# A hybrid layer's cache compression: ScalarE's work around a change of batch redistributed, and one addition moved to GpSimd

## The chip, the cores and the metric

The kernel runs on one core of a Trainium2 chip. The metric is the device time of one execution in microseconds, the median of three runs.

## The reference

The kernel computes one layer for a prompt of 1024 tokens and for 8 batches of 4 new tokens each, with a cache of 4096 past tokens. The layer has an HGRN2 mixer (a gated scan in chunks, 4 heads), a sparse attention (compressed blocks, selected blocks, window) and a feed-forward part with a convolution. What the change touches is the compression of cached keys and values, and the scan that runs beside it:

```python
def compress_rows(rows, pe, w1, w2):      # rows: (B, S, 2 groups, 64)
    ch = rows.reshape(B, n_chunks, 16, G, D)
    proj = jnp.einsum('bnsgd,psdh->pbngh', ch, w1)        # p: 2 halves of a block of 32
    bias = jnp.einsum('psd,psdh->ph', pe, w1)
    h = proj[0, :, 0:n_blk] + bias[0]
    h = h + proj[1, :, 1:1 + n_blk] + bias[1]
    return jnp.einsum('bngh,hd->bngd', jax.nn.silu(h), w2)

# the scan, in each chunk (C tokens), a = cumsum(log f):
att = einsum('bhtk,bhsk,bhtsk->bhts', q, k, exp(a_t - a_s))     # causal
o = att @ v + (q * exp(a)) @ s
s = exp(a_end) * s + (k * exp(a_end - a)).T @ v
```

## The kernel before, in words

The kernel is a sequence of stages. The one of this case is `compress_and_scan`. It has 72 steps: eight for each of the 8 batches of cached rows (64 steps, `PAIRS`), and eight for the prompt's rows. `at` is the step, `u = at // 8` the batch, `s = at % 8` the place in it. Each engine has its own program, written out by hand as a loop over the steps; semaphores tie them together. There is no planner.

In a step the engines prepare the data of step `at + 1` and TensorE multiplies those of step `at`:

- GpSimd gathers cached rows by an indirect DMA into one of 4 slots, three steps ahead (`gather`, line 2908).
- TensorE turns a slot into one bank, `pt`, three times (kinds 0 and 1: two halves of the rows to compress, kind 2: keys of the selection; line 3463). Each turn must wait until the bank is copied out.
- ScalarE and VectorE copy kind 0 out together (ScalarE two of four pieces, line 3156, VectorE two, `upper_copy`, line 3319), ScalarE copies kind 1 alone (four pieces, into `prow`). The result is `raw`. ScalarE then rounds it to a high part `XH` (line 3167), VectorE subtracts to get the low part `XL` (lines 3330 and 3332). For kind 0 the two halves of `raw` are also added in place (line 3333, VectorE) and split into `SH` (line 3175) and `SL`. For kind 2 the parts are `KTH` (line 3181) and `KTL` (line 3341), made by `keys`.
- TensorE runs `project_first` (with `XH`, `XL`, `SH`, `SL`), `project_second` in two halves, and `score`, into accumulators that are kept over the eight steps of a batch.

TensorE's order in a step is: turn 0 of the next step, `project_first`, turn 1, first half of `project_second`, `score`, turn 2, second half of `project_second`, with the products of the scan laid between. Turn 0 of step `at + 2` waits for the keys' low part of step `at + 1`.

At a change of batch, ScalarE copies the taps in step 7 (`keep_taps`, line 3115), VectorE joins them (`join_taps`, lines 3352 to 3354, six additions and subtractions that wait for each other), and in the next batch's step 0 ScalarE applies Silu: `hidden(u, 1)` straight from the accumulator, which TensorE needs before it may start the second projection, and `hidden(u, 0)` on the joined taps at the end of step 0 (both line 3132). Silu and Exp need a table load (1.28 us) whenever they take turns. In step 4 TensorE makes the compressed blocks (`blocks`, lines 3561 and 3568) into the bank of the scores, once ScalarE has copied the scores out (`keep_scores`, lines 3148 and 3149, every even step).

The scan takes one unit (a chunk of 128 tokens, or the new tokens) every two steps. GpSimd makes the differences of logarithms (`differences`, lines 2881 to 2885, 15 short instructions) and scales results (`scaled`), ScalarE takes exponentials (`exponentials`, odd steps), VectorE multiplies by keys and queries (`weigh`, part 0 at the end of an odd step, part 1 in the next even step), TensorE multiplies, VectorE masks and reduces (`pairs`, odd steps) to a tile `diag` of 128x32 whose four 32x32 blocks belong on the diagonal of `attT`. ScalarE copies them there (`diagonals`, line 3100), as its last work in the odd step; TensorE's `outputs` (line 3642), its last work in the odd step, waits for that.

SyncE stores values, loads the scan's chunks and, near the end of the stage, the next stage's tiles.

Of the kernel before, what the change touches and what calls it, by code (L numbers as in the profile page):

```python
# [2717 lines left out]
def compress_and_scan(nc, io, keep, scratch, consts_sb):  # L2718
# [11 lines left out]
    with ExitStack() as ctx:  # L2730
# [61 lines left out]
        raw_ready, upper_ready = [sem("raw_ready0"), sem("raw_ready1")], sem("upper_ready")  # L2792
        diag_kept = sem("diag_kept")
# [39 lines left out]

        def raw_whole(eng, at, k):
            eng.wait_ge(raw_ready[k], at + 1)
            if k == 0:
                eng.wait_ge(upper_ready, at + 1)
# [33 lines left out]
        def _(pool):  # L2871
# [38 lines left out]

            def add_scores(n):
                pool.wait_ge(s_kept, n + 1)
                nc.gpsimd.tensor_tensor(sx[:, n % 2, :], sx[:, n % 2, :], sxl[:], ALU.add).then_inc(s_added, 1)  # L2913

            differences(0)
            differences(1)
            pool.wait_ge(hc_in, 64)
            for at in range(LAST):
                if at + 3 < PAIRS:
                    gather(at + 3)  # L2920
                if at % 2 == 0:
                    if 2 <= at <= PAIRS:
                        add_scores(at // 2 - 1)
                    continue
                if at >= 2:
                    scaled(at // 2 - 1)
                if at // 2 + 2 < NN:
                    differences(at // 2 + 2)
# [148 lines left out]
        def _(act):  # L3077
# [16 lines left out]
            def diagonals(n):  # L3094
                if decode(n):
                    return
                act.wait_ge(a_kept, n + 1)
                for b in range(4):
                    x = slice(32 * b, 32 * b + 32)
                    last = nc.scalar.copy(attT[x, n % 2, x], diag[x, :])  # L3100
                last.then_inc(diag_kept, 1)

# [48 lines left out]
            def raw_copy(at, k):  # L3151
                act.wait_ge(t_ready[k], at + 1)
                if at >= 1:
                    act.wait_ge(l_ready[k], at)
                for g, a in parts[0:2] if k == 0 else parts:
                    last = nc.scalar.copy(part_of(raws[k], at, g, a), split(at, g, a))  # L3156
                last.then_inc(raw_ready[k], 1)
# [52 lines left out]
            for at in range(LAST):  # L3210
                u, s = at // NS, at % NS
                first_half(at + 1)
                if u >= 1 and s == 0:
                    hidden(u - 1, 1)
                if at % 2 == 0 and 2 <= at <= PAIRS:
                    keep_scores(at // 2 - 1)
                if s == NS - 1 and u < DB:
                    keep_taps(u)
                if at % 2 == 1 and at // 2 + 1 < NN:
                    exponentials(at // 2 + 1)  # L3220
                second_half(at + 1)
                if u >= 1 and s == 0:
                    hidden(u - 1, 0)
                if at % 2 == 1:
                    diagonals(at // 2)
                elif at >= 2:
                    squares(at // 2 - 1)
# [7 lines left out]
        def _(dve):  # L3235
# [24 lines left out]
            def pairs(n):  # L3260
# [12 lines left out]
                if n >= 1:  # L3273
                    dve.wait_ge(diag_kept, states(n - 1))
                nc.vector.tensor_reduce(diag[:], prod[:].rearrange("p l t -> p t l"), AX.X, ALU.add).then_inc(a_kept, 1)
# [34 lines left out]
            lows, boths = Steps(dve, low0_ready), Steps(dve, both_step)  # L3310

            def upper_copy(at):
                if at >= PAIRS:
                    return
                dve.wait_ge(t_ready[0], at + 1)
                if at >= 1:
                    dve.wait_ge(l_ready[0], at)
                for g, a in parts[2:4]:
                    last = nc.vector.tensor_copy(part_of(raws[0], at, g, a), split(at, g, a))
                last.then_inc(upper_ready, 1)  # L3320

            def low_part(at, k):
# [6 lines left out]
                elif k == 1:  # L3329
                    nc.vector.tensor_tensor(XL[:, at % 2, 1, :], raws[1], XH[:, at % 2, 1, :].bitcast(F32), ALU.subtract).then_inc(l_ready[1], 1)  # L3330
                else:
                    lows(nc.vector.tensor_tensor(XL[:, at % 2, 0, :], raw, XH[:, at % 2, 0, :].bitcast(F32), ALU.subtract))
                    nc.vector.tensor_tensor(raw[:, 0:256], raw[:, 0:256], raw[:, 256:512], ALU.add).then_inc(sum_ready, 1)
# [36 lines left out]
            upper_copy(0)  # L3370
# [31 lines left out]
            for at in range(LAST):  # L3402
                u, s = at // NS, at % NS
                n = at // 2
                if at + 1 < LAST:
                    upper_copy(at + 1)
                if at % 2 == 0:
                    if n >= 1 and not decode(n - 1):
                        results(n - 1)
                    weigh(n, 1)  # L3410
# [6 lines left out]
                if s == NS - 1 and u < DB:  # L3417
                    join_taps(u)
                if at + 1 < LAST:
                    low_part(at + 1, 1)  # L3420
                if at + 1 < PAIRS:
                    low_sum(at + 1)
                    keys(at + 1)
                if 1 <= u < DB - 1 and s == 1:
# [13 lines left out]
                if at % 2 == 1 and n + 1 < NN:  # L3438
# [8 lines left out]
        def _(pe):  # L3447
# [181 lines left out]
            def outputs(n):  # L3629
# [3 lines left out]
                pe.wait_ge(diag_kept, states(n))  # L3633
# [236 lines left out]
```

## Time and profile before

| | us |
|---|---|
| median of 3 runs | 2259.41 (2257.88 to 2262.35) |
| profiled execution, its own time | 2249.72 |
| its span | 2247.9 |
| TensorE busy (matmul) | 2066.3 |
| VectorE busy | 1441.2 |
| ScalarE busy | 1087.8 |
| GpSimd busy | 700.2 |

The span runs from the first to the last instruction of the profiled execution. The stage of this case lies between about 355 and 1041 us. A TensorE matmul's row has its duration in the pipeline; matmuls of 256 columns that follow each other start every 0.12 us.

### The profile page before, as it was taken

The numbers are of one execution on the slowest core, as the hardware profiler recorded it, in microseconds if no ns is written. First come the engines' busy times: TensorE is split into PE (matmuls) and PEld (weight loads), VectorE is DVE, ScalarE is ACT, GpSimd is POOL, SyncE is SP. The second block draws the span as 40 slices with busy tenths as digits, with TensorE's granted clock in tenths as the row PEclk, the third lists the DMA queues.
The fourth block names the chain that finished last, engine by engine and source line by source line (L and its number), as shares of the span: only waits on it lengthen the run. The fifth ranks groups of instructions, "written<-read, shape, count | busy, mean of one in ns | idle before, by whom it ended". The sixth has DMA issues, their size and how long they took to land. (4 is left out here: it accounts for less than half of the span.)

```text
span 2247.9 us, 44025 instructions
## 1 busy us (share of the span) xinstructions
PE 2066.3 (92%) x17158; PEld 1920.4 (85%) x17158; DVE 1441.2 (64%) x3058; ACT 1087.8 (48%) x2322; POOL 700.2 (31%) x996
## 2 busy tenths in 40 slices
PE   6999998998899889886789899898999999999997
PEld 5999997887888888874678777787999999999997
DVE  5212235776675766665678698548788788765567
ACT  4115214766766775764357487324333333334334
POOL 0001003655555654531059497120111111110000
PEclk9999999999999999976979899999999999999999
DMA  4115554765655655657610011331332332365352
GB/s 127 57 57 171 195 215 137 219 174 176 182 170 159 192 171 154 186 127 268 222 53 8 6 50 45 110 99 50 94 101 92 101 115 72 101 232 189 118 171 96
DMA packets 226055, 295.73 MB, mean 132 GB/s; under 512 B 23986, under 2 KB 161426, under 8 KB 224658
## 3 DMA queue, kind: packets, MB, share of 16 engines
q1 hardware_dynamic: 199224, 191.65, 28.1%
q0 software_dynamic: 26624, 101.27, 13.8%
q8 instruction: 137, 2.24, 0.4%
q14 instruction: 70, 0.57, 0.1%
HBM read 217.12 MB, written 82.63 MB: 133 GB/s over the span
## 5 line engine op out<-in xcount | busy, mean ns | idle before, releaser
L1568 POOL TENSOR_TENSOR C<-C,a_mt 128x264 f32<-128x264 f32 x66 | 69.3, 1070 | 404.1 <-ACT C L1653 270.4
L3520 PE MATMUL cplain<-a_XH,w1H 128*128 128x256 f32 x512 | 155.7, 304 | 12.2 <-ACT a_hs L3132 12.2
L2087 PE MATMUL f<-a_slot,wd_slot 128*128 128x264 f32 x1176 | 148.2, 285 | 2.0 <-DVE a_slot L1897 1.2
L2087 PEld LDWEIGHTS f<-a_slot,wd_slot 128*128 128x128 f32 x1176 | 144.8, 188 | 2.9 <-issue 1.9
L2050 PE MATMUL f<-a_b,ring 128*128 128x264 f32 x1056 | 144.1, 286 | 3.2 <-DVE a_b L1793 2.7
L3520 PE MATMUL cplain<-a_XL,w1H 128*128 128x256 f32 x512 | 145.0, 283 | 0.0
L3520 PE MATMUL cplain<-a_XH,w1L 128*128 128x256 f32 x512 | 144.6, 282 | 0.0
L3463 PE MATMUL cpt<-ident,X 128*128 128x128 f32 x768 | 119.1, 278 | 23.7 <-ACT a_prow L3156 19.5
L2050 PEld LDWEIGHTS f<-a_b,ring 128*128 128x128 f32 x1056 | 135.5, 190 | 3.8 <-issue 3.8
L502 PE MATMUL pj<-wH,xL 128*128 128x256 f32 (+2 forms) x464 | 130.9, 282 | 0.0
L502 PE MATMUL pj<-wH,xH 128*128 128x256 f32 (+2 forms) x464 | 130.8, 282 | 0.0
L502 PE MATMUL pj<-wL,xH 128*128 128x256 f32 (+2 forms) x464 | 130.5, 281 | 0.0
L2908 POOL DMA_INDIRECT X<-in_cache_nsa_kv,idx x122 | 118.6, 972 | 30.7 <-issue 25.0
L3463 PEld LDWEIGHTS cpt<-ident,X 128*128 128x128 f32 x768 | 88.2, 143 | 45.6 <-ACT a_prow L3156 36.1
L672 POOL TENSOR_SCALAR a_Prs<-a_Prs,a_cf 128x128 f32<-128x128 f32 (+7 forms) x64 | 110.5, 1746 | 17.0 <-DVE a_cf L817 16.9
L2050 PE MATMUL f<-b0a,ring 128*128 128x264 f32 x804 | 111.3, 289 | 1.5 <-ACT a_mt L1649 0.8
L3156 ACT COPY a_raw<-cpt 64x256 f32<-64x256 f32 x128 | 46.8, 366 | 132.9 <-PE cpt L3463 132.2
L3520 PEld LDWEIGHTS cplain<-a_XH,w1H 128*128 128x128 f32 x512 | 97.0, 189 | 15.0 <-issue 13.7
L2913 POOL TENSOR_TENSOR a_sx<-a_sx,a_sxl 64x512 f32<-64x512 f32 x32 | 48.3, 1511 | 196.1 <-ACT a_sxl L3149 196.1
L3156 ACT COPY a_prow<-cpt 64x256 f32<-64x256 f32 x256 | 93.6, 366 | 31.4 <-PE cpt L3463 28.6
L825 DVE TENSOR_TENSOR a_PTL<-pt,a_PTH 128x512 fp32r<-128x512 f32 x132 | 90.1, 688 | 28.1 <-ACT a_PTH L729 25.8
L2050 PE MATMUL f<-a_b,a_ring 128*128 128x264 f32 x792 | 106.7, 284 | 1.1 <-ACT a_mt L1649 0.6
(619 smaller groups left out, 6576.5 us busy)
## 6 DMA issues: line engine op xcount, KB each, us to landing
v_s<-X SPq DMA_DIRECT2D x64, 256.0 KB, 3.8
a_slot<-a_T SPq DMA_DIRECT2D x20, 792.0 KB, 4.6
raw<-in_w_in POOLq DMA_DIRECT2D x12, 1024.0 KB, 6.0
V<-v_s SPq DMA_DIRECT2D x6, 2048.0 KB, 11.2
raw<-in_w_gate SPq DMA_DIRECT2D x22, 512.0 KB, 5.2
raw_odd<-in_w_val SPq DMA_DIRECT2D x22, 512.0 KB, 5.6
a_T<-C SPq DMA_DIRECT2D x20, 528.0 KB, 3.2
a_T<-sums SPq DMA_DIRECT2D x11, 792.0 KB, 4.5
```

The costliest lines, as they stand in the source:

```text
L502: last = nc.tensor.matmul(bank[u % 8][0:r, 0:nw], xp[:, k, a * P:a * P + r], wp[:, j % 2, k, 0:nw], **flags)
L672: nc.gpsimd.tensor_scalar(Pr_of(u)[:, h, 0:u.w], Pr_of(u)[:, h, 0:u.w], cf[:, u.n, h:h + 1], None, ALU.mult).then_inc(p_ready, 1)
L825: nc.vector.tensor_tensor(lo, src, hi.bitcast(F32), ALU.subtract).then_inc(l_ready, 1)
L1568: nc.gpsimd.tensor_tensor(C[j][:, at], C[j][:, at], mt[:, q % 2, m, c], ALU.mult).then_inc(multiplied, 1)
L2050: last = nc.tensor.matmul(out_bank(q, r, c), w[:, k], x[:, k], start=begins and k + part == 0, stop=k == 3 and part == 2, skip_group_check ...
L2087: last = nc.tensor.matmul(acc(u, o, h), x(n)[:, k, P * o:P * o + P], a(n)[:, k, HW * h:HW * h + HW], start=u in (0, 2, 4, 6) and begins an ...
L2908: nc.gpsimd.indirect_dma_start(X[:, j % SLOTS, half].rearrange("p t n -> p (t n)"), None, cache, bass.IndirectOffsetOnAxis(ap=idx[:, j // ...
L2913: nc.gpsimd.tensor_tensor(sx[:, n % 2, :], sx[:, n % 2, :], sxl[:], ALU.add).then_inc(s_added, 1)
L3156: last = nc.scalar.copy(part_of(raws[k], at, g, a), split(at, g, a))
L3463: last = nc.tensor.transpose(pt[:, c:c + P], X[:, at % SLOTS, h, a, P * kind:P * kind + P], ident[:])
L3520: last = nc.tensor.matmul(out[:, h], w, x, start=(begins and q + h + part == 0), stop=(ends and q + h == 2 and part == 2), skip_group_chec ...
```

## The change

- The four copies of the diagonal blocks go from ScalarE (`diagonals`, removed with its semaphore) to VectorE, in `pairs`.
- The in-place addition of the two halves of `raw` goes from VectorE's `low_part` to GpSimd's new `row_sums`. GpSimd does it in each step after the gather and before the scores, the scaling and the differences.
- The copy of kind 1 out of the bank, which ScalarE did alone, is shared with VectorE for data of steps 1 and 2 of batches 1 to 7 (work done in steps 0 and 1).
- `hidden(u - 1, 0)` goes from the end of step 0 to step 1, behind the first half and ahead of the exponentials.
- In step 4 the scores are copied ahead of the first half, not after it.
- On VectorE `join_taps` goes from ahead of the last subtractions of step 7 to behind them; `weigh(n + 1, 0)`, which stood at the end of step 7, is done in step 0 behind `results`.

```diff
+        def shared(at, k):
+            return k == 0 or at >= NS and at % NS in (1, 2)
         def raw_whole(eng, at, k):
             eng.wait_ge(raw_ready[k], at + 1)
-            if k == 0:
-                eng.wait_ge(upper_ready, at + 1)
+            if shared(at, k):
+                eng.wait_ge(upper_ready[k], sum(shared(i, k) for i in range(at + 1)))
 # GpSimd
+            def row_sums(at):
+                if at >= PAIRS:
+                    return
+                pool.wait_ge(low0_ready, at + 1)
+                pool.wait_ge(h_ready[0], at + 1)
+                nc.gpsimd.tensor_tensor(raw[:, 0:256], raw[:, 0:256], raw[:, 256:512], ALU.add).then_inc(sum_ready, 1)
             differences(0)
+            row_sums(0)
             differences(1)
             for at in range(LAST):
                 if at + 3 < PAIRS:
                     gather(at + 3)
+                row_sums(at + 1)
                 if at % 2 == 0:
 # ScalarE
-            def diagonals(n):
...
-                for g, a in parts[0:2] if k == 0 else parts:
+                for g, a in parts[0:2] if shared(at, k) else parts:
...
+                scores_due = at % 2 == 0 and 2 <= at <= PAIRS
+                if scores_due and s == 4:
+                    keep_scores(at // 2 - 1)
                 first_half(at + 1)
                 if u >= 1 and s == 0:
                     hidden(u - 1, 1)
-                if at % 2 == 0 and 2 <= at <= PAIRS:
+                if scores_due and s != 4:
                     keep_scores(at // 2 - 1)
+                if u >= 1 and s == 1:
+                    hidden(u - 1, 0)
                 if s == NS - 1 and u < DB:
                     keep_taps(u)
                 if at % 2 == 1 and at // 2 + 1 < NN:
                     exponentials(at // 2 + 1)
                 second_half(at + 1)
-                if u >= 1 and s == 0:
-                    hidden(u - 1, 0)
-                if at % 2 == 1:
-                    diagonals(at // 2)
-                elif at >= 2:
+                if at % 2 == 0 and at >= 2:
                     squares(at // 2 - 1)
 # VectorE
-                if n >= 1:
-                    dve.wait_ge(diag_kept, states(n - 1))
-                nc.vector.tensor_reduce(diag[:], prod[:].rearrange("p l t -> p t l"), AX.X, ALU.add).then_inc(a_kept, 1)
+                posts(nc.vector.tensor_reduce(diag[:], prod[:].rearrange("p l t -> p t l"), AX.X, ALU.add))
+                for b in range(4):
+                    r = slice(32 * b, 32 * b + 32)
+                    last = nc.vector.tensor_copy(t[r, r], diag[r, :])
+                last.then_inc(a_kept, 1)
...
-            def upper_copy(at):
-                if at >= PAIRS:
+            def upper_copy(at, k):
+                if at >= PAIRS or not shared(at, k):
                     return
...
-                    lows(nc.vector.tensor_tensor(XL[:, at % 2, 0, :], raw, XH[:, at % 2, 0, :].bitcast(F32), ALU.subtract))
-                    nc.vector.tensor_tensor(raw[:, 0:256], raw[:, 0:256], raw[:, 256:512], ALU.add).then_inc(sum_ready, 1)
+                    nc.vector.tensor_tensor(XL[:, at % 2, 0, :], raw, XH[:, at % 2, 0, :].bitcast(F32), ALU.subtract).then_inc(low0_ready, 1)
...
                     if n >= 1 and not decode(n - 1):
                         results(n - 1)
+                    if u >= 1 and s == 0:
+                        weigh(n, 0)
                     weigh(n, 1)
...
-                if s == NS - 1 and u < DB:
-                    join_taps(u)
                 if at + 1 < LAST:
+                    upper_copy(at + 1, 1)
                     low_part(at + 1, 1)
                 if at + 1 < PAIRS:
                     low_sum(at + 1)
                     keys(at + 1)
+                if s == NS - 1 and u < DB:
+                    join_taps(u)
...
-                if at % 2 == 1 and n + 1 < NN:
+                if at % 2 == 1 and n + 1 < NN and s < NS - 1:
                     weigh(n + 1, 0)
 # TensorE, outputs
                 pe.wait_ge(a_kept, n + 1)
-                pe.wait_ge(diag_kept, states(n))
```

## Rows read from the trace of the kernel before

**Rows 1.** TensorE's waits, 355 to 1060 us: waiting, releaser, total us, times, longest.

```profile
PE cpt L3463 <- ACT a_prow L3156: 19.5, 21, 1.5
...
PE chg L3642 <- ACT a_attT L3100: 13.1, 32, 2.2
PE cplain L3520 <- ACT a_hs L3132: 12.2, 7, 1.8
...
PE cst L3561 <- ACT a_sxl L3149: 4.9, 7, 0.8
```

**Rows 2.** TensorE's timeline: start us, duration us, instruction, idle before and releaser.

```profile
431.32 0.60 PE L3463 MATMUL cpt<-ident,X 128*128 128x128 f32 x4
...
441.06 0.60 PE L3463 MATMUL cpt<-ident,X 128*128 128x128 f32 x4
...
445.99 0.36 PE L3520 MATMUL cplain<-a_XH,w1H 128*128 128x256 f32 x1 [1.75 <-ACT a_hs L3132]
...
448.48 0.66 PE L3463 MATMUL cpt<-ident,X 128*128 128x128 f32 x4 [0.35 <-ACT a_prow L3156]
...
458.14 0.66 PE L3463 MATMUL cpt<-ident,X 128*128 128x128 f32 x4 [1.22 <-ACT a_prow L3156]
...
461.34 0.60 PE L3463 MATMUL cpt<-ident,X 128*128 128x128 f32 x4
...
469.56 0.60 PE L3463 MATMUL cpt<-ident,X 128*128 128x128 f32 x4
...
477.65 0.60 PE L3463 MATMUL cpt<-ident,X 128*128 128x128 f32 x4
```

**Rows 3.** ScalarE's timeline, steps 0, 1 and 3.

```profile
442.64 0.62 ACT L3167 CAST a_XH<-a_raw 128x512 fp32r<-128x512 f32 x1 [0.20 <-ACT a_raw L3156]
...
449.89 1.34 ACT L3132 ACTIVATE a_hs<-a_hs,a_bias 128x512 f32<-128x512 f32 x2
...
456.60 1.49 ACT L3156 COPY a_prow<-cpt 64x256 f32<-64x256 f32 x4
...
475.87 0.89 ACT L3100 COPY a_attT<-a_diag 32x32 f32<-32x32 f32 x4
```

**Rows 4.** VectorE's timeline, steps 7, 0, 1, 2 and 3.

```profile
435.45 0.52 DVE L3352 TENSOR_TENSOR a_both<-a_hs 128x256 f32<-128x256 f32 x1
...
438.50 0.69 DVE L3330 TENSOR_TENSOR a_XL<-a_prow,a_XH 128x512 fp32r<-128x512 f32 x1 [0.17 <-ACT a_XH L3167]
...
440.04 0.21 DVE L3246 TENSOR_TENSOR a_W<-a_W,a_akq 128x64 f32<-128x64 f32 x1
...
441.70 0.87 DVE L3319 COPY a_raw<-cpt 64x256 f32<-64x256 f32 x2 [0.50 <-PE cpt L3463]
...
453.90 0.37 DVE L3271 COPY a_attT<-chg 32x32 f32<-32x32 f32 x2
...
465.28 1.40 DVE L3333 TENSOR_TENSOR a_raw<-a_raw 128x256 f32<-128x256 f32 x1
...
467.78 0.68 DVE L3341 TENSOR_TENSOR a_KTL<-cpt,a_KTH 128x512 fp32r<-128x512 f32 x1
...
472.63 0.68 DVE L3332 TENSOR_TENSOR a_XL<-a_raw,a_XH 128x512 fp32r<-128x512 f32 x1
```

**Rows 5.** GpSimd's timeline, steps 0 to 3.

```profile
446.98 1.28 POOL L2913 TENSOR_TENSOR a_sx<-a_sx,a_sxl 64x512 f32<-64x512 f32 x1 [7.92 <-ACT a_sxl L3149]
...
468.77 0.47 POOL L2898 TENSOR_TENSOR a_gin<-a_gin,a_normw 128x128 f32<-128x128 f32 x1
...
474.68 0.98 POOL L2908 DMA_INDIRECT X<-in_cache_nsa_kv,idx  x1
475.97 0.96 POOL L2908 DMA_INDIRECT X<-in_cache_nsa_kv,idx  x1 [0.30 <-issue]
```

**Rows 6.** Windows: length, busy time by engine, granted clock (PEclk), DMA share, GB/s.

```profile
540.00:544.00 4.00, 4.00 (x23) 4.00 (x22) 3.94 (x22) 1.81 (x4) 0.00 (x0) 0.57 0.00 0
444.00:448.00 4.00, 2.25 (x17) 1.75 (x15) 1.39 (x4) 3.93 (x8) 1.02 (x1) 1.00 0.90 320
```

More of the change, by code:

```diff
@@ L2791, in compress_and_scan @@
         low0_ready, sum_ready, sumH_ready = (sem(n) for n in ("low0_ready", "sum_ready", "sumH_ready"))
-        raw_ready, upper_ready = [sem("raw_ready0"), sem("raw_ready1")], sem("upper_ready")
-        diag_kept = sem("diag_kept")
+        raw_ready, upper_ready = ([sem(f"{n}{k}") for k in range(2)] for n in ("raw_ready", "upper_ready"))
         h_ready, l_ready, mm_ready = ([sem(f"{n}{k}") for k in range(2)] for n in ("h_ready", "l_ready", "mm_ready"))
@@ L3092, in exponentials @@
                 nc.scalar.activation(KE[:, n % 2, 0:r], KE[:, n % 2, 0:r], ACT.Exp).then_inc(exp_ready, 1)
-            def diagonals(n):
[L3095 to L3101, printed above, removed]
             def squares(n):
@@ L3308, in keep_blocks @@
                 nc.vector.tensor_copy(kvc[:], st[:]).then_inc(c_kept, 1)
-            lows, boths = Steps(dve, low0_ready), Steps(dve, both_step)
-            def upper_copy(at):
-                if at >= PAIRS:
+            boths = Steps(dve, both_step)
+            def upper_copy(at, k):
+                if at >= PAIRS or not shared(at, k):
                     return
-                dve.wait_ge(t_ready[0], at + 1)
+                dve.wait_ge(t_ready[k], at + 1)
                 if at >= 1:
-                    dve.wait_ge(l_ready[0], at)
+                    dve.wait_ge(l_ready[k], at)
                 for g, a in parts[2:4]:
-                    last = nc.vector.tensor_copy(part_of(raws[0], at, g, a), split(at, g, a))
-                last.then_inc(upper_ready, 1)
+                    last = nc.vector.tensor_copy(part_of(raws[k], at, g, a), split(at, g, a))
+                last.then_inc(upper_ready[k], 1)
             def low_part(at, k):
@@ L3368, in queries @@
                 nc.vector.tensor_tensor(qpS[:, u % 2, 96:128], qblk[:, u, :], qpH[:, u % 2, 32:64].bitcast(F32), ALU.subtract).then_inc(qp_ready, 1)
-            upper_copy(0)
+            upper_copy(0, 0)
             low_part(0, 0)
@@ L3405, in _ @@
                 if at + 1 < LAST:
-                    upper_copy(at + 1)
+                    upper_copy(at + 1, 0)
                 if at % 2 == 0:
```

## The prediction

> **What bounds the kernel now.** The change touches only the stage that compresses the cache, some 690 of the 2248 us. I read first the list of waits of that stretch. TensorE has almost no wait for data from memory there. Its waits are for copies on ScalarE: 19.5 us for the copies that clear the transpose bank (21 waits), 13.1 us for the diagonal blocks (32 waits), 12.2 us for the hidden activation at a change of batch (7 waits), 4.9 us for kept scores (7 waits) [rows 1]. Between them its matmuls follow each other without a gap, so in this stage a microsecond taken from a wait is a microsecond of the kernel, unless the next wait takes it back. Then I read TensorE's timeline over one change of batch and over an ordinary pair of steps [rows 2]. The reader should take from it where each step (0 to 7 of a batch) begins: step 7 at 431.32, step 0 at 441.06, step 2 at 461.34, step 3 at 469.56, step 4 at 477.65. ScalarE, VectorE and GpSimd over the same time [rows 3 to 5] show who lets it go on.
>
> **Diagonals.** ScalarE's four copies (0.89 us) are the last thing of an odd step [rows 3]. They go; VectorE does four of the same size right after its reduction. Of the 13.1 us of waits one is 2.2 us long [rows 1]; the other 31 share 10.9 us, 0.35 us each, and all of it goes: VectorE makes its blocks about 3 us before TensorE asks for them (the subtraction behind them starts at 472.63, TensorE is at the outputs 4 us later) [rows 2, 4]. At step 7, however, the next thing is late for another reason (below), so 7 of the 31 bring nothing. Gain: 24 x 0.35 = 8.4 us. The price on VectorE: two copies of 32x32 take 0.37 us [rows 4], so four, with the wait for the reduction, about 0.6 us, in steps where VectorE then waits for ScalarE anyway: nothing by itself.
>
> **Scores at step 4.** The copies of the scores now stand ahead of step 4's first half, where ScalarE is idle since the diagonals are gone. The 7 waits, 4.9 us, go [rows 1]. Nothing waits longer: what stands behind them is a copy that only becomes possible at the start of step 4. Gain: 4.9 us.
>
> **Joining the taps.** This is moved on VectorE from ahead of the last subtractions of step 7 to behind them. It took from 435.45 to 438.33 (the next instruction starts at 438.50 after 0.17 us idle): 2.9 us. In the new place it starts where the weighing now starts, 440.04, and ends at 442.9; only then comes the copy out of the transpose bank that began at 441.70. So this copy, 0.87 us, ends at 443.8 and not at 442.6: 1.2 us later [rows 4]. Behind it on ScalarE hang the cast at 442.64, the table load and the hidden activation, and TensorE starts its second projection 3.35 us after that cast starts, at 445.99 [rows 2, 3]. It will start 1.2 us later. The weighing that is taken out of step 7 (8 short products) lies behind the copy in step 0 and delays nothing: its keys and products are wanted three microseconds later.
>
> **The shared copy.** In steps 0 and 1 ScalarE makes two of the four copies out of the bank, half of 1.49 us [rows 3], VectorE the others (0.87 us, like its two now [rows 4]) in time in which it idles. In step 0 that takes away the wait ahead of the turned keys, 0.35 us idle, 0.5 us with the drained pipeline ahead of it [rows 2]. Step 0: +1.2 - 0.5 = +0.7 us.
>
> **Hidden activation in step 1.** Its 1.34 us (the next instruction starts 1.24 us after it) move from the end of step 0, where ScalarE then idled, to ahead of the exponentials of step 1, where TensorE already waits 1.22 us for ScalarE at 458.14 [rows 2, 3]. Against it stands the half copy, 0.75 us. Step 1: +0.5 us. The number of table loads stays as it is. With 7 changes of batch: 7 x (0.7 + 0.5) = +8.4 us.
>
> **The sum on GpSimd.** VectorE's addition, 1.40 us in even steps [rows 4], is replaced by one on GpSimd, which no row shows. GpSimd's addition of 128x128 takes 0.47 us and of 64x512 1.28 us when nothing is in its way [rows 5]; between them lies about 0.75 us, the value I take; the ends are 0.47 and 1.28. In odd steps VectorE's subtraction ends at 472.63 + 0.68, with the diagonals 0.6 us later, 473.9; the sum ends at 474.7, when ScalarE is just coming for it. Behind it GpSimd's queue holds the scaling, the differences and two gathers, from 468.77 to 476.9, 8.2 us [rows 5]. They now start at 474.7 and end at 482.9, 5.6 us into the even step (which begins 0.35 us earlier than 477.65). Its sum then ends 6.3 us into the step; VectorE's ended at 5.3 us (465.28 + 1.40 against 461.34) [rows 2, 4]. One microsecond late, it meets a slack of 1.1 us: the last subtraction of the keys ends at 468.46, the next step begins at 469.56 [rows 2, 4]. Only even steps behind an odd step of ordinary length are touched: step 6 of seven batches and three steps of the first, less one behind a short unit, 9 in all. The gathers come 5 us later than now, with three steps (some 24 us) until their data are used, and no wait for them is among the large ones: nothing; SyncE's queue keeps its order. What is unknown is how GpSimd's differences, which now lie beside VectorE's weighing, and that weighing slow each other. Low end: nothing. High end: 1 us in each of 16 even steps, 16 us, by the in-place addition that took 1.40 us beside GpSimd's add. I take +2 us, near the low end, since the instructions concerned are short ones.
>
> The Trainium skill ("SBUF — State Buffer", section "SBUF: two separate sides") says that VectorE with two SBUF inputs and GpSimd take a shared port pair in turn, the one that comes second waiting out the whole instruction of the first. That 1.40 us sum agrees. By this rule the second rival below would be the likelier outcome.
>
> **The tail of the stage** (prompt rows) has one wait of 2.2 us for the diagonals that goes, and the joining moved behind the subtractions, worth up to 2.4 us the other way. I take nothing; ends -2 and +2.
>
> **Sum:** -8.4 - 4.9 + 8.4 + 2 = -2.9 us, say -3. The profiled execution took 2249.7 us (span 2247.9 and 1.8 around it), so 2246.7; the median shown is 9.7 above it, so 2256 us.
>
> **Rivals.**
> 1. *The batch change is cheaper than I make it.* If the joining does not reach the path (its 2.9 us shrink beside an idle GpSimd, or TensorE comes late anyway), 7 x 1.2 us and the 7 x 0.35 us of step 7 stay in hand: -3 - 10.9 = -14 us, 2246. For it: the edit spreads ScalarE's work just where the three longest waits stand. Against it: VectorE has only 0.50 us idle ahead of 441.70 [rows 4], and 2.9 us are put there for 1.2 taken away. With half of that, -8 us.
> 2. *GpSimd and VectorE pay for each other.* The sum comes one more microsecond late, or the weighing pushes the copy behind it, in 9 to 16 even steps at 0.6 to 0.8 us: +5 to +12 on the base of -5: 2260 to 2267, middle 2263. For it: ScalarE's chain in an even step is as long as TensorE's time to it. Against it: the instructions are short. It decides once the queue of 8.2 us grows beyond 8.3.
> 3. *TensorE's clock falls at each change of batch.* The idle time ahead of its second projection grows from 1.75 to some 2.9 us. At 1.75 us the granted clock stays at 1.00; after a wait and a sparse stretch around 539 it is at 0.57 for 4 us, a mixture of 2.4 and 1.2 GHz [rows 6]. That costs 4 x 0.43 = 1.7 us, seven times 12 us: -3 + 12 = +9, 2268, slower than now. It decides from the length of idle time at which the clock falls, which lies somewhere above 1.75 us. The Trainium skill ("TensorE: Matmul & The Clock Gate", section "HAM oscillation — how this bites in real kernels") describes kernels that fall back to the lower clock in every tile for a wait in it; this case's trace shows it only after sparse stretches.
>
> **Chances.** Forecast 0.40, first rival 0.18, second 0.24, third 0.18. The forecast's own range is 2251 to 2261. For all, 2246 to 2271: below it remains the full first rival at most, above it rivals 2 and 3 together. A difference of 0.2% (4.5 us) is about what can be told from none. Faster by more: 0.22 of the forecast and 0.18 of the first rival, 0.40. Within: 0.17 of the forecast and 0.07 of the second, 0.24. Slower: 0.36, from the second and third.
>
> **What the changed profile would show.** TensorE's waits for the diagonal blocks and ahead of the blocks of step 4 gone, none for VectorE in their place. At a change of batch the wait for the hidden activation at about 2.9 us and not 1.75; the one in step 1 ahead of the turned keys about 1.7 and not 1.22; that of step 7 still near 1.46 us (19.5 us in [rows 1] hardly smaller). GpSimd's sum at about 0.75 us, and step 6 as long as now. I am wrong if the hidden activation's wait does not grow (then rival 1), if even steps grow beyond 8.3 us with ScalarE waiting for GpSimd's sum (rival 2), or if the granted clock drops behind that wait (rival 3).

## The result: slower by 1.4%, and the profile after

| | before | after |
|---|---|---|
| median of runs, us | 2260.88 (4 runs, 2257.88 to 2266.59) | 2292.88 (4 runs, 2283.98 to 2293.80) |
| profiled execution, its time; span, us | 2249.72; 2247.9 | 2292.33; 2290.5 |
| 70 steps of the stage in that execution, us | 648.6 | 685.8 |

The ratio is 1.014, 95% interval 1.0114 to 1.0166. The forecast was 2256, its range ended at 2271: wrong in sign and outside the range. Of the 42.6 us between the two profiled executions 37.2 lie in the stage's 70 steps, counted on TensorE's timeline: a step begins with the block of turns `cpt` that stands ahead of `ctaps`. The other 5.4 us lie outside the stage: in the kernels profiled below the span less these 70 steps varies from 1599 to 1615 us, and the kernel before is at the low end. So steps are compared for the stage, each from one profiled execution, and medians for the whole.

The core's span and mean granted clock in the kernel after (before: 2247.9 us, 0.964):

```profile
core 0: 2290.5 us, clock 0.956
```

TensorE's waits of the kernel after, 355 to 1060 us (waiting, releaser, total us, times, longest), to be held against [rows 1]:

```profile
PE cpt L3470 <- ACT a_prow L3158: 29.5, 28, 1.7
PE cplain L3527 <- ACT a_hs L3134: 18.0, 7, 2.6
...
PE cpt L3470 <- DVE a_KTL L3345: 7.1, 6, 2.8
...
PE cjoint L3509 <- DVE a_hs L3358: 3.3, 6, 0.6
PE cpt L3470 <- DVE a_raw L3324: 3.3, 5, 1.1
```

The two waits that the change was to remove are gone: no row for the diagonal blocks (13.1 us) and none for the kept scores (4.9 us). But the copies on ScalarE are waited for 10 us more, the hidden activation 5.8 us more, and three rows name VectorE. (A further row, for VectorE's `a_XL`, grew from 5.8 to 12.6 us; it belongs to the stage's last steps, which grew by 1.9 us in all.) TensorE's timeline over the same change of batch follows, to be held against [rows 2]. Step 0 begins at 447.38, step 1 at 461.99, step 2 at 471.50, step 3 at 481.21, and step 4, which is used below, at 488.97:

```profile
447.38 0.62 PE L3470 MATMUL cpt<-ident,X 128*128 128x128 f32 x4
450.00 0.51 PE L3509 MATMUL cjoint<-a_SH,ws 128*128 128x256 f32 x2 [0.57 <-DVE a_hs L3358]
...
454.26 0.55 PE L3527 MATMUL cplain<-a_XH,w1H 128*128 128x256 f32 x1 [2.64 <-ACT a_hs L3134]
...
461.99 0.27 PE L3470 MATMUL cpt<-ident,X 128*128 128x128 f32 x1
...
468.78 0.66 PE L3470 MATMUL cpt<-ident,X 128*128 128x128 f32 x4 [1.69 <-ACT a_prow L3158]
471.50 0.63 PE L3470 MATMUL cpt<-ident,X 128*128 128x128 f32 x4
...
481.21 0.60 PE L3470 MATMUL cpt<-ident,X 128*128 128x128 f32 x4
```

The step lengths, summed over the stage and set beside the forecast's terms, tell where the time went:

| steps | forecast, us | measured, us |
|---|---|---|
| 1, 3 and 5 (diagonals gone; first hidden half in step 1) | -8.4 + 3.5 = -4.9 | -3.4 |
| 4 of seven batches (scores) | -4.9 | -5.2 |
| 0 of seven batches (joining, shared copy) | +4.9 | +23.8 |
| 2 and 6, and 0 and 4 of the first batch (sum on GpSimd; see below for the diagonals' share) | +2 | +19.7 |
| 7 | 0 | +0.5 |
| the last seven | 0 | +1.9 |
| all | -3 (rounded) | +37 |

Two rows of the table carry the miss. The first is step 0, and three windows of the kernel after show it (columns as in [rows 6]). TensorE does nothing from 452 to 454 us; the granted clock leaves 1.00 there and is 0.50, that is 1.2 GHz, for the four microseconds behind. The matmuls of 256 columns then start every 0.21 us instead of 0.12:

```profile
452.00:454.00 2.00, 0.00 (x0) 0.00 (x0) 2.00 (x13) 1.99 (x3) 0.36 (x1) 0.80 1.02 295
454.00:458.00 4.00, 3.74 (x15) 3.47 (x16) 2.20 (x5) 2.81 (x7) 3.33 (x3) 0.50 0.98 300
458.00:462.00 4.00, 4.00 (x73) 3.30 (x72) 0.69 (x1) 0.89 (x3) 1.07 (x2) 0.75 1.09 379
```

The second is that of the even steps. It can be read at the start of step 4 of the same batch, where TensorE's turns begin at 488.97 us. VectorE's timeline of the kernel after (start, duration):

```profile
488.15 0.68 DVE L3345 TENSOR_TENSOR a_KTL<-cpt,a_KTH 128x512 fp32r<-128x512 f32 x1
488.75 0.21 DVE L3249 TENSOR_TENSOR a_W<-a_W,a_akq 128x64 f32<-128x64 f32 x1
488.88 0.33 DVE L3250 TENSOR_TENSOR a_W<-a_W,a_akq 128x64 f32<-128x64 f32 x1
489.14 0.33 DVE L3249 TENSOR_TENSOR a_W<-a_W,a_akq 128x64 f32<-128x64 f32 x1
...
490.42 0.36 DVE L3250 TENSOR_TENSOR a_W<-a_W,a_akq 128x64 f32<-128x64 f32 x1
490.79 0.87 DVE L3324 COPY a_raw<-cpt 64x256 f32<-64x256 f32 x2
```

and GpSimd's at that time:

```profile
485.93 0.73 POOL L2918 TENSOR_TENSOR a_raw<-a_raw 128x256 f32<-128x256 f32 x1 [4.36 <-DVE a_XL L3337]
486.61 0.46 POOL L2900 TENSOR_TENSOR a_gin<-a_gin,a_normw 128x128 f32<-128x128 f32 x1
487.15 0.79 POOL L2901 TENSOR_TENSOR a_ob<-a_ob,a_gin 128x128 f32<-128x128 f32 x1
487.91 0.47 POOL L2883 TENSOR_TENSOR a_W<-a_akq 128x64 f32<-128x64 f32 x1
488.34 0.29 POOL L2884 TENSOR_TENSOR a_W<-a_akq 128x64 f32<-128x64 f32 x1
488.59 0.28 POOL L2883 TENSOR_TENSOR a_W<-a_akq 128x64 f32<-128x64 f32 x1
488.84 0.29 POOL L2884 TENSOR_TENSOR a_W<-a_akq 128x64 f32<-128x64 f32 x1
```

The sum takes 0.73 us, as forecast. But GpSimd waited 4.36 us for VectorE's subtraction before it could make it, and its queue is in order: scaling and the 14 differences start behind it. They now run while VectorE weighs, and from the second on the eight weighings follow each other every 0.26 us, the pace of GpSimd's differences, instead of every 0.13. The same stretch in the kernel before, at the start of the same step (477.65):

```profile
476.04 0.69 DVE L3341 TENSOR_TENSOR a_KTL<-cpt,a_KTH 128x512 fp32r<-128x512 f32 x1
476.64 0.22 DVE L3246 TENSOR_TENSOR a_W<-a_W,a_akq 128x64 f32<-128x64 f32 x1
...
477.58 0.21 DVE L3247 TENSOR_TENSOR a_W<-a_W,a_akq 128x64 f32<-128x64 f32 x1
478.29 0.87 DVE L3319 COPY a_raw<-cpt 64x256 f32<-64x256 f32 x2 [0.49 <-PE cpt L3463]
```

Before, weighing is over when the turns are there, and VectorE waits 0.49 us for them. After, the copy starts 1.8 us behind the start of the turns instead of 0.64: 1.2 us later, and ScalarE's cast of these rows with it. Two things make up the 1.2 us. The weighings begin 0.22 us ahead of the turns where they had begun 1.02 us ahead, 0.8 us later; the kernel with the diagonals alone, below, has most of this too (0.31 us ahead). And they take 0.9 us longer by GpSimd's pace; the 0.49 us that VectorE idled are used up.

The cast's waits in ScalarE's list of the kernel after, for which the profile names no releaser (before: 5.0 us, 3 times; some 14 of the 47 us belong to step 0 at the seven changes of batch):

```profile
ACT a_XH L3169 <- issue: 47.0, 29, 2.3
```

It is not the weighings alone. VectorE's subtraction for the second half of the rows (`XL` from `prow`) takes 0.69 us in the mean before. After, it takes 0.97 us in the mean of 63 steps, more than 1 us in ten of them, and 3.67 us in one, where it begins among GpSimd's differences and ends behind the last of them (VectorE's and GpSimd's row of the kernel after):

```profile
936.61 3.67 DVE L3335 TENSOR_TENSOR a_XL<-a_prow,a_XH 128x512 fp32r<-128x512 f32 x1 [2.53 <-ACT a_XH L3169]
...
939.34 0.39 POOL L2887 TENSOR_TENSOR a_KE<-a_akq 128x128 f32<-128x128 f32 x1
```

The Trainium skill ("SBUF — State Buffer", section "A bandwidth-pool intuition that's wrong (but worth ruling out)") says that when two operations slow each other in this memory, one is stalled and the two do not share bandwidth. The trace agrees, since only one of the two gets slower: VectorE's pace becomes GpSimd's 0.25 us from start to start, while GpSimd's differences keep that pace in most rows.

### The profile page after: what moved, and what is told of

It reads as the page before. It is cut to its first block and busy times, and to the rows that moved or that the text cites. A ratio compares the mean times of both kernels' runs of the same rounds, so it can differ in the third digit from the quotient of the medians.

```text
span 2290.5 us, 44085 instructions
## 1 busy us (share of the span) xinstructions
PE 2087.2 (91%) x17158; PEld 1937.3 (85%) x17158; DVE 1470.6 (64%) x3150; ACT 1053.1 (46%) x2166; POOL 750.3 (33%) x1060
## 5 line engine op out<-in xcount | busy, mean ns | idle before, releaser
L3470 PE MATMUL cpt<-ident,X 128*128 128x128 f32 x768 | 124.2, 286 | 44.8 <-ACT a_prow L3158 29.5
L2910 POOL DMA_INDIRECT X<-in_cache_nsa_kv,idx x122 | 131.6, 1078 | 31.0 <-issue 25.6
L3335 DVE TENSOR_TENSOR a_XL<-a_prow,a_XH 128x512 fp32r<-128x512 f32 x64 | 62.2, 971 | 104.9 <-ACT a_XH L3169 104.8
L2918 POOL TENSOR_TENSOR a_raw<-a_raw 128x256 f32<-128x256 f32 x64 | 47.5, 742 | 219.1 <-DVE a_XL L3337 218.9
L3527 PEld LDWEIGHTS cplain<-a_XH,w1H 128*128 128x128 f32 x512 | 100.9, 197 | 20.8 <-issue 19.5
```

What stands on the lines that cost most here:

```text
L2910: nc.gpsimd.indirect_dma_start(X[:, j % SLOTS, half].rearrange("p t n -> p (t n)"), None, cache, bass.IndirectOffsetOnAxis(ap=idx[:, j // ...
L2918: nc.gpsimd.tensor_tensor(raw[:, 0:256], raw[:, 0:256], raw[:, 256:512], ALU.add).then_inc(sum_ready, 1)
L3470: last = nc.tensor.transpose(pt[:, c:c + P], X[:, at % SLOTS, h, a, P * kind:P * kind + P], ident[:])
L3527: last = nc.tensor.matmul(out[:, h], w, x, start=(begins and q + h + part == 0), stop=(ends and q + h == 2 and part == 2), skip_group_chec ...
```

## The experiments

"Stage" is the change of the 70 steps against the kernel before, in one profiled execution of each kernel. The ratio compares the runs with runs of the kernel before taken beside them, with its 95% interval; it is not exactly the ratio of the medians. Beside the twelve experiments, in the table's order, the kernel before had medians of 2258.41 (first four), 2259.61 (next four) and 2260.5 us (last four).

| kernel | stage, us | median, us | ratio |
|---|---|---|---|
| after | +37.2 | 2292.88 | 1.014 (1.0114 to 1.0166) |
| joining back | +12.4 | 2266.42 | 1.0042 (1.0019 to 1.0064) |
| sum back | +6.5 | 2266.04 | 1.0035 (1.0014 to 1.0055) |
| joining, sum, weighing back | -3.9 | 2252.48 | 0.9976 (0.9953 to 1.0000) |
| after, 20 dummy products | +35.8 | 2297.67 | 1.0168 (1.0121 to 1.0215) |
| after, 12 dummy products | +26.6 | 2281.27 | 1.0092 (1.0056 to 1.0127) |
| joining and sum back, GpSimd's wait kept | +9.0 | 2271.00 | 1.0036 (1.0013 to 1.0059) |
| before, diagonals alone | +1.7 | 2260.76 | 0.9999 (0.9981 to 1.0016) |
| reordered | -6.4 | 2254.50 | 0.9983 (0.9963 to 1.0003) |
| joining back, GpSimd's sum queued later | +2.2 | 2261.42 | 1.0002 (0.9981 to 1.0024) |
| before, sum on GpSimd alone | +26.8 | 2280.99 | 1.0100 (1.0067 to 1.0133) |
| diagonals alone, 8 dummy products | -3.4 | 2254.07 | 0.9976 (0.9956 to 0.9996) |
| reordered, copy not shared | -29.2 | 2233.14 | 0.9887 (0.9850 to 0.9925) |

**The joining back ahead of the last subtractions** (half 0's weighing stays in step 0, the sum on GpSimd).

```
                     low_part(at + 1, 0)
+                if s == NS - 1 and u < DB:
+                    join_taps(u)
                     upper_copy(at + 1, 1)
...
-                if s == NS - 1 and u < DB:
-                    join_taps(u)
```

> The changed kernel with join_taps put back ahead of the last subtractions of step 7, all else as changed (GpSimd's sum stays). Theory A (two causes: the late joining, which lengthens TensorE's wait at the change of batch to 2.64 us and with it drops its clock to 1.2 GHz; and GpSimd's differences beside VectorE's weighing in even steps): step 0 shrinks from 14.6 to about 11 us, no fall of the clock there, 7 x 3.6 = 25 us less, about 2268 us; even steps stay at 9.5 us. Theory B (the clock falls there for another reason): only the wait shrinks, 7 x 1.2 = 8 us, about 2284.

Measured 2266.42. The hidden wait is 1.74 us again in six batches (0.22 in the seventh), the clock stays at 1.00 behind it, and step 0 takes 10.2 us in six of seven batches, against 10.77 before and 13.6 to 14.7 after. Even steps stay at 9.5 to 9.7. So in the kernel after it is the joining's place that makes step 0's loss, with the sum still on GpSimd.

**The sum back on VectorE** (GpSimd's `row_sums` gone, the addition behind the subtraction of half 0 again).

> The changed kernel with the sum of even and odd rows back on VectorE, all else as changed. Theory A: steps 2 and 6 (and 2, 4, 6 of the first batch) go from 9.5-9.7 us back to 8.2, VectorE's weighing from 1.8 back to 1.1 us, some 18 x 1.3 = 24 us less, about 2269; step 0 stays at 14.6 us. Theory C (even steps are long through another part of the change, such as the diagonal copies on VectorE): no difference, 2293.

Measured 2266.04: even steps of 8.4 to 8.8 us, where 8.2 was expected, and step 0 still 13.2 to 14.5 with the clock falling. What is left in the even steps, 5.1 us in all, is what the kernel with the diagonals alone, below, shows too. The odd steps 1, 3 and 5 lose another 5.6 us. Each loss goes when its own edit is undone, 24.8 and 30.7 us of the stage. That is more than 37.2 together, so the two are not independent.

**Both back, and half 0's weighing back at the end of step 7.**

> The changed kernel with both put back, and with the weighing at the end of step 7 again: what is left are the diagonals on VectorE, the scores first in step 4, the shared copy in steps 0 and 1 and the hidden activation in step 1. Theory A: the two effects add, 25 + 24 us less than the changed kernel, about 2244, some 16 us under the kernel before. If the two overlap (one wait hides the other), between 2250 and 2265.

Measured 2252.48, where 2244 was expected; in the stage 41.1 us are undone and not 24.8 + 30.7. Six of the seven hidden waits are 2.02 to 2.03 us instead of 1.75, and in five of these batches step 0 takes 12.0 instead of the 10.5 that the sixth shows: the clock falls again, at a wait only 0.28 us longer than before. The kernels that leave the weighing in step 0, with the joining back, have 1.74 or 1.75 us there (two of them 0.2 us in one batch), whether the sum is on GpSimd or not; so this part of the change, which the forecast took for neutral, seems to have helped by 9 us in step 0. No kernel changes it alone.

**Dummy products in TensorE's wait**, to take the clock away and leave the wait: 20, then 12.

```
                 turn(at + 1, 1)
+                if 1 <= u < DB and s == 0:
+                    pe.wait_ge(o_kept, n)
+                    pe.wait_ge(s_ready2, states(n - 1))
+                    for _ in range(20):          # the second kernel: 12
+                        nc.tensor.matmul(hg[:, 448:512], ident[:], ident[:, 0:64], start=True, stop=True)
```

> The changed kernel in which TensorE makes 20 small products that nobody reads (identity by 64 columns, into a free part of a bank) while it waits for the hidden activation in step 0. The wait for ScalarE stays as long. Theory A: the granted clock stays at 1.0 behind it, the second projection and what follows take 2.4 us less at each of 7 changes of batch, 17 us less, about 2276. If the slow matmuls there have another cause than idle time: 2293 or a little more.

Measured 2297.67, a miss: 20 products took 4.46 us, more than the wait of 2.64 us, and pushed the projection itself back by 1.8 us. But the clock held (kernel with 20, windows as above):

```profile
449.00:453.00 4.00, 3.87 (x31) 3.54 (x32) 3.92 (x22) 2.94 (x4) 2.01 (x3) 1.00 1.04 347
453.00:457.00 4.00, 4.00 (x35) 3.96 (x35) 2.31 (x5) 2.92 (x7) 3.22 (x3) 1.00 1.03 286
```

and from the start of the second projection to the end of the step it took 5.3 us instead of 7.7 (other batches: 6.7 to 7.9, without the second, which is longer in every kernel).

> The changed kernel with 12 dummy products (64 columns each, into an unused stretch of a PSUM tile, results never read) that TensorE makes in its wait at the start of step 0, about 2.7 us by the duration that 20 of them took (4.46 us). The wait is 2.64 + 0.57 us, so they fit into it. Theory (the fall of TensorE's clock after the wait costs about 2.4 us per batch change): the granted clock stays at 1.00, step 0 goes from 14.6 to about 12.2, seven times: -17, about 2276. Rival (what stretches step 0 is what its steps wait for and the clock only shows it): products at full speed wait elsewhere instead, 2293 within 0.2%.

Measured 2281.27, with 2276 expected and 2293 for the rival. The second projection starts 6.86 us into step 0 as without them (6.88), so the wait is as long, and the clock is 1.00 in all seven. Step 0 falls from 14.6 to 12.1 us; over the seven batches it loses 14.0 us, 2.0 each (three of them took only 13.6 and so had less to lose). That is the clock's part of step 0's +23.8; the other 9.8 us are the longer waits.

**GpSimd waits as for its sum, but VectorE makes the sum** (and the joining is back).

```
-                nc.gpsimd.tensor_tensor(raw[:, 0:256], raw[:, 0:256], raw[:, 256:512], ALU.add).then_inc(sum_ready, 1)
+                # only: pool.wait_ge(low0_ready, at + 1)
```

> The changed kernel with the joining ahead of the last subtractions again and the sum of even and odd rows on VectorE again, but GpSimd still waits for the subtraction of half 0 at the places where it made the sum; beside the kernel with the same two edits without that wait, and beside the kernel where GpSimd makes the sum (2266, even steps 9.5 to 9.7). Theory A (the place of GpSimd's differences is what costs: the wait holds them until VectorE weighs, and the two slow each other down): even steps stay near 9.5, about 2263. Theory B (what costs is the sum on GpSimd itself, 0.74 us for 0.4, and its lateness): even steps fall to about 8.5, about 2247.

Measured 2271.00, even steps mostly 9.4 us: theory A. GpSimd does less here than in the kernel after, and VectorE's addition takes 0.42 us where it had taken 0.79 in the mean of the kernel before; yet the steps are nearly as long. The weighings show why (VectorE of this kernel):

```profile
484.23 0.33 DVE L3248 TENSOR_TENSOR a_W<-a_W,a_akq 128x64 f32<-128x64 f32 x1
...
485.27 0.33 DVE L3248 TENSOR_TENSOR a_W<-a_W,a_akq 128x64 f32<-128x64 f32 x1
485.62 0.87 DVE L3322 COPY a_raw<-cpt 64x256 f32<-64x256 f32 x2
```

The kernel with both back (and the weighing, which touches steps 7 and 0 only) is the one without the wait. Steps 2 and 6 (with those of the first batch, as in the table above) are 4.3 us over the kernel before there, 17.4 us here, and 20.0 with the sum itself on GpSimd. So 13.1 of 15.7 us come from the wait in front of the differences, and at most 2.7 from who makes the sum.

**GpSimd's sum behind the differences** in odd steps (joining back).

```
-                row_sums(at + 1)
                 if at % 2 == 0:
+                    row_sums(at + 1)
...
                     differences(at // 2 + 2)
+                row_sums(at + 1)
```

> The changed kernel with the joining ahead of the last subtractions again, and in odd steps GpSimd's addition queued behind the results' scaling and the 14 differences instead of ahead of them; in even steps it stays. Beside the same kernel with the addition in front (2266, even steps 9.5 to 9.7). Theory A (the wait of the addition for VectorE holds the differences back until VectorE weighs, and it is there that the two slow each other): the differences run a step earlier, as before, weighing takes 0.14 us from one to the next again, even steps fall to about 8.5, about -18: 2248. Theory B (an addition on GpSimd is late and slow wherever it stands): even steps stay at 9.5 or odd steps grow by what even steps lose, 2266 or more.

Measured 2261.42, between the two. Weighings follow every 0.14 us again and even steps fall to 8.3 to 8.8, as theory A has it. But some odd steps (step 3 in six batches) grow from 7.8 to 8.8 us, as theory B has it. TensorE waits there for the keys' low part, which VectorE makes behind what needs the sum:

```profile
484.46 0.63 PE L3471 MATMUL cpt<-ident,X 128*128 128x128 f32 x4 [1.16 <-DVE a_KTL L3346]
```

**The sum alone on GpSimd**, in the kernel before.

> The kernel before with only the addition of even and odd rows moved to GpSimd, at the places where the change put it. Theory A (this part alone makes the even steps 1.2 us longer): even steps from 8.2 to about 9.4, 18 of them, odd steps unchanged at 8.1: about +22, 2282. Rival (the even steps grow only together with the diagonals' copies on VectorE): 2260 to 2265.

Measured 2280.99, near theory A's number, but that is luck, since the sum is another one. The ordinary steps 2 and 6 grow mostly by 0.4 to 0.85 us, not 1.2, and these and the even steps of the first batch by 10.4 us in all. Step 0 grows by 8.6 us: the hidden wait is 2.0 to 2.6 us in six batches, and the clock falls in five of seven. The steps 4 grow by 7.7 us, as the wait for kept scores grows (9.5 us for 4.9); 4.6 of that are one step 4, where this wait is 2.31 us and the clock is 0.50 for the nine microseconds behind it. In an ordinary even step the copy out of the bank starts 1.22 us behind the turns here, 0.87 with the diagonals alone, 1.81 with both and 0.64 before: the 1.2 us come from both together.

**The diagonals alone**, in the kernel before.

> The kernel before with only the diagonals' copies moved to VectorE. By the steps of the changed kernel (odd steps 8.10 to 7.77 in 24 steps) about -8: 2250. Rival (VectorE, with four more copies in odd steps, delays the even steps' subtractions and gives the gain back): 2257 to 2262.

Measured 2260.76, no gain. Odd steps 1, 3 and 5 get shorter by 11.4 us in all, 0.59 each. Steps 2, 4 and 6 give back 5.6 us and step 7 1.7 us: VectorE's four copies take 0.94 us, 1.1 with the wait for the reduction, not 0.6. And step 0 gives back 6.3 (0.8 of it in the first batch), since the hidden wait is now 2.02 us in six batches and the clock falls behind four of them:

```profile
446.26 0.49 PE L3510 MATMUL cplain<-a_XH,w1H 128*128 128x256 f32 x1 [2.02 <-ACT a_hs L3122]
...
448.00:452.00 4.00, 4.00 (x43) 3.43 (x42) 1.72 (x3) 3.23 (x7) 2.42 (x3) 0.78 0.46 86
```

> The kernel with only the diagonals' copies moved to VectorE (2260.8), with 8 dummy products (64 columns each, about 1.8 us) that TensorE makes in its wait of 2.02 us in step 0. Theory (the gain of the diagonals went into a fall of TensorE's clock, since the wait is 2.02 us instead of 1.75): the granted clock stays at 1.00, step 0 falls from 12.0 to about 10.8 in six batches, -8: 2253. Rival (the stage's steps are held by VectorE, the clock is beside the point): 2260.

With eight dummy products in that wait step 0 is 11.08 us in the ordinary batches (before them up to 12.02) and the kernel takes 2254.07, as the theory has it (2253); the interval of its ratio to the kernel before ends just below 1.

**Reordered**: sum and joining back, half 0's hidden activation back at the end of step 0, half 1's ahead of the first copies of step 0; diagonals, scores, shared copies and the late weighing as in the change.

```
+                if u >= 1 and s == 0:
+                    hidden(u - 1, 1)
                 first_half(at + 1)
```

> The changed kernel with the sum of even and odd rows back on VectorE, the joining ahead of the last subtractions of step 7 again, ScalarE's first hidden half back at the end of step 0, the weighing of half 0 left in step 0 (where the change put it), and ScalarE's second hidden half ahead of its first copies in step 0. What it keeps: diagonals on VectorE, scores ahead of the copies at step 4, shared copies. Theory (each part costs what its steps showed): odd steps -8, step 4 -5, and step 0 no longer waits for the hidden rows (2 us per batch change, -14) and step 1 loses part of its 9.5: in all about 2230. Rival (the copies that the hidden half goes ahead of are the next wait and take all of it): 2246.

Measured 2254.50, a miss. The hidden wait is gone from TensorE's list, and in its place stands VectorE's shared copy (13 waits, 23.1 us). In step 0 it is 2.3 to 2.4 us in six batches, and the clock falls behind four of them. On VectorE that copy queues behind an addition that takes 1.37 us beside GpSimd's:

```profile
447.33 1.37 DVE L3329 TENSOR_TENSOR a_raw<-a_raw 128x256 f32<-128x256 f32 x1
448.73 0.87 DVE L3315 COPY a_prow<-cpt 64x256 f32<-64x256 f32 x2
```

**The same without sharing that copy.**

```
-            return k == 0 or at >= NS and at % NS in (1, 2)
+            return k == 0
```

> The kernel with the sum and the joining back, hidden half 0 back, half 1 ahead of the first copies (2254.5, where TensorE waits 2.35 us in step 0 for VectorE's copy of half 1 and the clock falls to 0.72 to 0.85), with that copy back on ScalarE (1.49 us instead of 2 x 0.73). Theory (the copy is late since it stands behind an addition of 1.37 us on VectorE, and the clock falls by the long wait): TensorE waits under 1.5 us, the clock stays at 1.00, step 0 falls from 11.8 to about 9.5, -16: 2238. Rival (ScalarE is as late with its own copy): 2254 to 2262.

Measured 2233.14: faster than before by 1.1% (0.75 to 1.5), than the kernel after by 2.6%. Step 0 takes 8.3 to 8.7 us in six of seven batches (before 10.77), its longest wait is 0.22 us and the clock stays at 1.00:

```profile
446.95 0.66 PE L3462 MATMUL cpt<-ident,X 128*128 128x128 f32 x4 [0.22 <-ACT a_prow L3149]
...
444.00:448.00 4.00, 3.78 (x48) 3.13 (x46) 3.97 (x17) 3.44 (x8) 2.40 (x2) 1.00 1.01 345
448.00:452.00 4.00, 4.00 (x80) 3.77 (x67) 2.69 (x7) 3.37 (x9) 3.04 (x6) 1.00 0.72 170
```

## Why the prediction was wrong, point by point

The term that failed most is the sum on GpSimd, taken at +2 us: alone it costs 26.8 us in the stage, and undone it gives 30.7. The next is the joining at 7 x 1.2 us, with the clock's fall left out of the sum: step 0 was forecast at +4.9 us and came to +23.8. Point by point:

- **What bounds the stage**: right. TensorE's waits set its length; over the 13 kernels of the table the medians moved by what the stage moved, within 6.4 us.
- **Diagonals**: 0.33 us in each of steps 3 and 5, 0.35 forecast, but the match is luck. With the diagonals alone, or with the sum back, these steps take 7.51 us for 8.10: the gain is 0.59, since the outputs now follow the product before them in 0.13 us and not in 0.64, of which only 0.35 are idle. The forecast counted such a drained pipeline for the shared copy, but not here. The sum on GpSimd took 0.26 back. "Nothing by itself" on VectorE was wrong: with the diagonals alone everything was given back, and 5.1 of the +19.7 us in the even steps are theirs.
- **Scores at step 4**: right (-5.2, forecast -4.9).
- **Shared copy and hidden activation in step 1**: right. Step 1 takes 9.39 us in the kernel with joining, sum and weighing back, against 8.91 with the diagonals alone: +0.48, forecast +0.5; its wait in the kernel after is 1.69 us (forecast 1.7). Where the clock holds, step 0 of the same two kernels is 10.50 against 11.07 us: -0.57, forecast -0.5.
- **Joining the taps**: the mechanism was right, the size not. The joining took 2.8 us (forecast 2.9) and the second projection starts 3.34 us after the cast (3.35). But it starts 0.24 us ahead of the turns, where the weighing had started 1.02 us ahead [rows 2, 4]: the turns come sooner without the diagonals' wait, and VectorE's subtractions come later beside GpSimd. The cast is thus 2.0 us later against the turns and not 1.2. TensorE also waits 0.57 us for the bank that the joining clears, which the forecast had not looked at. Without the clock step 0 came out 1.4 us longer (9.8 us in seven), forecast 0.7.
- **The clock** was left out of the sum, as rival 3 with a chance of 0.18. The forecast itself made the wait 2.9 us, and no row showed a fall or none at such a length; the runs did, behind every one of the 14 waits of 2.64 or 2.65 us. The rival's price (12 us) was near the 14.0 measured.
- **The sum on GpSimd**: this step failed most. +2 was taken, with a high end of 16. Undone, it gives 14.6 us in steps 2 and 6 (the fourth row of the table of step lengths), 5.6 in steps 1, 3 and 5, 4.6 in step 7 and 5.9 elsewhere. The forecast saw that the differences would come to lie beside the weighing, and took the near end "since the instructions concerned are short ones". Short ones are no exception: eight of them follow GpSimd's pace, 0.12 us lost nearly eight times, and what stands behind them is the copy for which ScalarE waits at once. It looked for the loss where the sum's own result is wanted; within the steps ScalarE waited for that once, 1.6 us.
- **Chances**: rivals 2 and 3 were weighed as alternatives. Nothing in them excludes the other, and both came. The range, which ends at 2271, left the two together outside: at their own prices they give 2263 + 12 = 2275, and 2292.88 was measured. Of the profile it was also forecast that no wait for VectorE would come in the place of those that go, and that the waits for the bank's copies (19.5 us) would stay; three rows name VectorE, and the copies came to 29.5.

How much each part is worth next to the others: undoing the joining takes 24.8 us off the stage, undoing the sum 30.7, both (with the weighing) 41.1. The shared copy, the hidden activation in step 1 and the weighing's new place were not tried alone.

## What to carry to other kernels

A wait added to an in-order queue can cost more by what stands behind it than by the instruction that waits: list what will now run at a later time, and beside what. Here a train of short operations on VectorE beside one on GpSimd ran at GpSimd's pace, and a longer one once waited until the train was over. And when an edit lengthens a wait of TensorE from 1.75 us to 2 or more, as here, put the fall of the clock into the sum. Before moving work, see whether the order within the step can shorten that wait: here that took 16.6 us off the seven steps 0 against the kernel before, more than any of the moves.

## What the runs showed of the hardware

- The granted clock fell behind more of the waits the longer they were, and no single length separates the two. I read the granted clock of the 9 us from the start of each second projection on. Behind waits of 1.74 or 1.75 us it was 1.00 in 28 of 29, and 0.81 in the one that remains (the second change of batch of the kernel with the sum alone on GpSimd). Behind 2.02 to 2.03 us it was 0.81 in 10 of 13 and 1.00 in three. Behind 2.35 us (the sum alone) it was 1.00 in two of four, and behind the waits of 2.3 to 2.4 us for the shared copy in the reordered kernel in two of six. Behind 2.64 or 2.65 us it was 0.66 to 0.84 in all 14 (six of the kernel after, seven with the sum back, one with the sum alone), and behind 2.16 us 0.82 in the kernel after. In some batches the fall came at once (0.21 us from matmul to matmul), in others some microseconds later.
- Dummy products in a wait held the clock, and twelve of 64 columns cost nothing in six of seven waits (0.3 us in the wait of 2.16 us, which they overran); 20 did not fit. Each took 0.22 us (4.46 us for 20, 2.69 us for 12).
- An addition of 128x256 on VectorE took 0.42 to 0.43 us in most steps, and 1.37 to 1.55 us in 24 of 64 in the kernel before, beside GpSimd's addition of 64x512, which itself went from 1.28 to 1.6 or 1.7 us there. GpSimd's own of 128x256 took 0.74 us in the mean of 64.
- The time outside the stage varied by 16 us between profiled executions of kernels that are alike there; the runs of the kernel before spread by 20 us. What varies was not looked into.
